# A hybrid mLSTM and attention layer on one core: output weights loaded during the attention and split during the mLSTM's first chunks

## The reference

```python
h = rmsnorm(x, norm1_w) * (1 + sc1) + sh1
mq, mk, mv, mo, mi, mf, sq, sk, sv = split_proj(h @ w_in)
...
ml_new, h_cell = mlstm_prompt(q_a, k_a, v_a, ig, lf)        # 4 heads x 128, chunkwise
y_a = rmsnorm(h_cell, ml_norm_w) * sigmoid(mo)
o_b = stick_breaking(q_b, k_all, v_all)                     # 8 heads x 64, 128-query blocks
y_b = rmsnorm(o_b, sb_out_norm_w)
mix = jnp.concatenate([y_a, y_b], axis=-1) @ w_out          # w_out: 1024 x 1024
x = x + g1 * mix
h2 = rmsnorm(x, norm2_w) * (1 + sc2) + sh2
x = x + g2 * (conv_ffn(h2) @ w_down)
```

## Time and profile before

| | |
|---|---|
| median of 3 runs (lowest to highest) | 3388.79 us (3387.54 to 3391.09) |
| the profiled execution's own time | 3391.34 us |
| its span, first to last instruction | 3389.7 us |
| mean granted TensorE clock | 0.968 of full speed |
| PE / PEld busy | 3178.1 (94%) / 2797.1 (83%) us |
| DVE / ACT / POOL busy | 1531.8 (45%) / 1076.4 (32%) / 749.2 (22%) us |
| DMA | 335.88 MB, mean 99 GB/s |

### The profile page before, as it was taken

One profiled execution on the slowest core, in us unless ns is written; L12 is line 12 of the kernel. 1 busy time (PEld: TensorE's weight loads), 2 busy tenths in 40 slices (PEclk: granted clock), 3 DMA queues, 4 the chain that ended last, 5 costly groups with the idle time before them and its releaser, 6 DMA issues. The chain is left out here.

```text
span 3389.7 us, 45737 instructions
## 1 busy us (share of the span) xinstructions
PE 3178.1 (94%) x17258; PEld 2797.1 (83%) x17258; DVE 1531.8 (45%) x1986; ACT 1076.4 (32%) x2064; POOL 749.2 (22%) x665
## 2 busy tenths in 40 slices
PE   7999999996999999896996999999999994999999
PEld 3877777774998999675885999999999994887786
DVE  1300000554988899574652544444444444324322
ACT  3611111222776777223553221222122212112111
POOL 3311101222665666001110111111111112002000
PEclk9999999997999999897997999999999997999999
DMA  5312211336522340564544111111111114335332
GB/s 184 114 66 67 68 62 66 127 125 156 133 52 52 67 83 9 185 231 178 180 159 158 50 50 50 37 38 50 50 50 50 50 38 151 139 117 173 139 138 70
DMA packets 247992, 335.88 MB, mean 99 GB/s; under 512 B 58093, under 2 KB 170153, under 8 KB 240685
## 3 DMA queue, kind: packets, MB, share of 16 engines
q1 hardware_dynamic: 231662, 284.75, 27.5%
q0 software_dynamic: 14864, 49.31, 4.4%
q10 hardware_dynamic: 1332, 0.06, 0.0%
HBM read 225.16 MB, written 108.89 MB: 99 GB/s over the span
## 5 line engine op out<-in xcount | busy, mean ns | idle before, releaser
L1770 PE MATMUL facc<-h2H,fwH 128*128 128x416 f32 x1760 | 617.8, 351 | 25.4 <-DVE h2L L1719 25.4
L1770 PE MATMUL facc<-h2L,fwH 128*128 128x416 f32 x1760 | 617.5, 351 | 0.0
L1770 PE MATMUL facc<-h2H,fwL 128*128 128x416 f32 x1760 | 617.3, 351 | 0.0
L644 PE MATMUL pacc<-pring,h1H 128*128 128x512 f32 x1360 | 453.0, 401 | 18.6 <-POOL pring L520 12.7
L941 POOL TENSOR_TENSOR aS<-aS,aC 128x512 f32<-128x512 f32 (+3 forms) x326 | 334.2, 1031 | 199.7 <-DVE aC L903 196.5
L903 DVE TENSOR_TENSOR_SCAN aC<-aB,aC,a 128x512 f32<-128x512 f32 (+3 forms) x326 | 362.7, 1113 | 24.2 <-ACT aB L878 17.8
L1662 ACT ACTIVATE fU<-facc 128x416 f32<-128x416 f32 (+1 forms) x220 | 113.1, 514 | 788.4 <-PE facc L1770 788.4
L1736 DVE TENSOR_SCALAR fV<-fU,fcw,fcb 128x2048 f32<-128x2048 f32 x88 | 112.3, 1318 | 536.8 <-ACT fU L1664 536.7
L1770 PEld LDWEIGHTS facc<-h2H,fwH 128*128 128x128 f32 x1760 | 331.1, 188 | 28.7 <-issue 26.1
L1770 PEld LDWEIGHTS facc<-h2H,fwL 128*128 128x128 f32 x1760 | 331.1, 188 | 2.7
L1770 PEld LDWEIGHTS facc<-h2L,fwH 128*128 128x128 f32 x1760 | 331.2, 188 | 2.5
(11 more groups left out here) (265 smaller groups left out, 4745.8 us busy)
## 6 DMA issues: line engine op xcount, KB each, us to landing
da<-act_d SPq DMA_DIRECT2D x32, 1408.0 KB, 7.0
proj_out<-pstage SPq DMA_DIRECT2D x119, 256.0 KB, 2.0
fraw<-w_up SPq DMA_DIRECT2D x44, 512.0 KB, 5.7
act_d<-fV SPq DMA_DIRECT2D x22, 1024.0 KB, 5.3
qk_T<-pturn POOLq DMA_DIRECT2D x68, 256.0 KB, 3.0
aq<-qk_T SPq DMA_DIRECT2D x32, 512.0 KB, 12.1
mwa<-w_ada SPq DMA_DIRECT2D x16, 1024.0 KB, 5.5
praw<-w_in SPq DMA_DIRECT2D x56, 256.0 KB, 2.8
```

The costliest lines, as they stand in the source:

```text
L644: op = mm_(acc[:, n % NB], h[:, kk, tok(t)], weight(q, w), start=(kk == 0 and part == 0), stop=(kk == KD - 1 and part == 2))
L1770: mm = nc.tensor.matmul(dst, a[:, j, kk], h[:, kk, cols], start=(kk == 0 and m == 0), stop=(kk == KD - 1 and m == 2))
```

## The change

- `w_out` becomes a tile that lives from the attention to the end of the mLSTM. In the attention its 32 KB per partition first hold `xk`, `xq` and `blank` (11 of 16 pieces). When the sync engine comes to row 0 of head 3, behind that row's store, it waits until the cached keys and queries are turned and the blank rows stored, and loads `w_out` there.
- In the mLSTM two tiles are added, `oH` and `oL`. ScalarE copies four parts ahead of its work on chunk 0 and four ahead of that on chunk 1; POOL makes four low parts ahead of its wait for chunk 0's result and four ahead of that for chunk 1's. The load of `w_out` at the end is gone, and the modulation's bias is loaded into the tile of its rows and added in place.
- The output projection gets `oH` and `oL` instead of `w_out`; its splitting and the waits for it are gone. Tile 0 is loaded first, then the norm weights, tiles 1 and 2, and last the gate rows, which have their own semaphore, waited for ahead of the first `finish`.

```diff
@@ attention
-        xq = sbuf(nc, s, "bxq", [P, W5])
-        xk = sbuf(nc, s, "bxk", [P, NPB1, W5])
+        spare = w_out[:].rearrange("p k (a n) -> p (k a) n", n=W5)
+        xk, xq, blank = spare[:, 0:NPB1], spare[:, NPB1], spare[:, NPB1 + 1]
...
                 store(scored[m])
                 if kind == PROMPT and (h, i) == (0, NPT // 2):
                     load_sample()
+                if kind == PROMPT and (h, i) == (3, 0):
+                    sp.wait_ge(turned, max(x for x in range(N) if items[x][0] in (KEYS, QUERIES)) + 1)
+                    sp.wait_ge(blank_stored, 16)
+                    sp.dma_start(w_out[:], d["w_out"].rearrange("(k p) n -> p k n", p=P)).then_inc(w_out_in, 16)
...
+            sp.wait_ge(w_out_in, 16)
@@ mlstm
-        bias = sbuf(nc, s, "mbias", [2, NM * P])
...
             tiles(sp, body)
-            sp.dma_start(w_out[:], d["w_out"].rearrange("(k p) n -> p k n", p=P)).then_inc(w_out_in, 16)
-            sp.wait_ge(w_out_in, 16)
             sp.wait_ge(mod_row, NPT)
...
             def body(t, u, r, first):
+                if isinstance(t, int) and t in (0, 1):
+                    for kk in range(t * KD // 2, (t + 1) * KD // 2):
+                        pool.wait_ge(o_high, kk + 1)
+                        nc.gpsimd.tensor_tensor(oL[:, kk], w_out[:, kk], oH[:, kk].bitcast(F32), ALU.subtract).then_inc(o_low, 1)
                 pool.wait_ge(h_ready, t + 1)
...
             def body(t, u, r, first):
+                if isinstance(t, int) and t in (0, 1):
+                    for kk in range(t * KD // 2, (t + 1) * KD // 2):
+                        nc.scalar.activation(oH[:, kk], w_out[:, kk], ACT.Copy).then_inc(o_high, 1)
                 act.wait_ge(qkv_in[u], 48 * r + 48)
...
-                v.tensor_tensor(mod_rows[:, span], pm[0:2, 0:2 * P], bias[:, span], ALU.add).then_inc(mod_row, 1)
+                v.tensor_tensor(mod_rows[:, span], pm[0:2, 0:2 * P], mod_rows[:, span], ALU.add).then_inc(mod_row, 1)
@@ output_projection
-            for n in range(2):
-                src = d["mods"][n:n + 1, (2 * KD - NMOD) * P:(3 * KD - NMOD) * P]
-                sp.dma_start(gate[:, n], src.to_broadcast([P, D])).then_inc(rows_in, 16)
-            sp.dma_start(wrow[:], d["y_norms"]).then_inc(rows_in, 16)
...
-            for t in range(3):
+            load(Turn(0, 0, 0))
+            sp.dma_start(wrow[:], d["y_norms"]).then_inc(rows_in, 16)
+            for t in range(1, 3):
                 load(Turn(t, t, 0))
+            for n in range(2):
+                src = d["mods"][n:n + 1, (2 * KD - NMOD) * P:(3 * KD - NMOD) * P]
+                sp.dma_start(gate[:, n], src.to_broadcast([P, D])).then_inc(gate_in, 16)
             turns_of_four(sp, slot)
...
-            for kk in range(0, KD, 2):
-                weights_split(pool, kk)
...
-            for kk in range(KD):
-                nc.scalar.activation(wH[:, kk], raw[:, kk], ACT.Copy).then_inc(w_high, 1)
...
-            dve.wait_ge(rows_in, 48)
-
-            for kk in range(1, KD, 2):
-                weights_split(dve, kk)
+            dve.wait_ge(rows_in, 16)
...
+                if first(i):
+                    dve.wait_ge(gate_in, 32)
                 dve.wait_ge(mix_ready, i.t + 1)
...
-                        if isinstance(i.t, int) and i.t == 0 and half == 0:
-                            pe.wait_ge(w_low[kk % 2], kk // 2 + 1)
```

More of the change, by code:

```diff
@@ L710, in _, with attention @@
                 turn(m)
-def attention(k, c):
+def attention(k, c, w_out):
     nc, d = k.nc, k.d
@@ L737, in attention @@
     (edge_set, nought_set, z_ready, pass_ready, stop_ready, left_ready, w_ready, turned, av_done, o_taken, past_k_in, past_v_in,
[L738 removed]
+     sample_set, sample_stored, blank_stored, w_out_in) = k.sems(
         "edge_set", "nought_set", "z_ready", "pass_ready", "stop_ready", "left_ready", "weight_ready", "weight_turned",
[L740 removed]
+        "av_done", "o_taken", "past_k_loaded", "past_v_loaded", "sample_tiles_set", "sample_stored", "blank_stored",
+        "w_out_loaded")
     taken = [k.sem("turned_taken_by_act"), k.sem("turned_taken_by_dve")]
@@ L821, in load_sample @@
                 own = tok(NPT)
-                sp.dma_start(xq[:], d["proj_out"][5, own, :]).then_inc(past_k_in, 16)
+                sp.dma_start(xq, d["proj_out"][5, own, :]).then_inc(past_k_in, 16)
                 for x, g, cache, sem in ((xk, 6, "past_k", past_k_in), (vs, 3, "past_v", past_v_in)):
@@ L932, in _ @@
             nc.gpsimd.memset(qs[:], 0.0).then_inc(sample_set, 1)
-            nc.gpsimd.memset(blank[:], 0.0).then_inc(sample_set, 1)
+            nc.gpsimd.memset(blank, 0.0).then_inc(sample_set, 1)
             nc.gpsimd.tensor_copy(far_s[:], c["far_r"][:, 0:DEC].bitcast(F32).unsqueeze(1).to_broadcast([P, 4, DEC])
@@ L1004, in _, with mlstm @@
                 scores(av, n - 6)
-def mlstm(k, c, gc, dec, w_out):
+def mlstm(k, c, gc, dec, w_out, oH, oL):
     nc, d = k.nc, k.d
@@ L1070, in _ @@
             sp.dma_start(C[1][:], d["c_init"]).then_inc(state_in, 16)
-            sp.dma_start(bias[:], d["b_ada"][:, NMOD * P:].to_broadcast([2, NM * P])).then_inc(bias_in, 16)
+            sp.dma_start(mod_rows[:], d["b_ada"][:, NMOD * P:].to_broadcast([2, NM * P])).then_inc(bias_in, 16)
             def body(t, u, r, first):
@@ L1301, in _, with output_projection @@
             mm.then_inc(mod_turned, 1)
-def output_projection(k, c, raw):
+def output_projection(k, c, wH, wL):
     nc, d = k.nc, k.d
@@ L2011, in build @@
         k.end_phase()
-        attention(k, c)
-        k.end_phase()
         with ExitStack() as s:
             w_out = sbuf(nc, s, "w_out_sb", [P, KD, D])
-            mlstm(k, c, gc, dec, w_out)
+            attention(k, c, w_out)
             k.end_phase()
-            output_projection(k, c, w_out)
+            oH = sbuf(nc, s, "w_out_high", [P, KD, D], F32R)
+            oL = sbuf(nc, s, "w_out_low", [P, KD, D], F32R)
+            mlstm(k, c, gc, dec, w_out, oH, oL)
+            k.end_phase()
+            output_projection(k, c, oH, oL)
             k.end_phase()
```

18 lines of the change are left out of this document (5 added, 13 removed).

## The result

The changed kernel takes **3404.55 us** (median of 8 runs, 3397.37 to 3408.79), the kernel before in the same comparison 3389.89 (8 runs, 3387.54 to 3391.47). The ratio is 1.0041, with a 95% interval of 1.0030 to 1.0051: slower, by some 14.7 us. The forecast was 3391.2 with a range to 3398.5, and "the same" as the likeliest case. It was wrong.

What follows compares the result with a forecast made beforehand. The prediction took TensorE's pace to bound each stage once going. Its terms, -5.9 + 5.5 + 2.8 = +2.4 us, made the profiled 3391.34 into 3393.7, and the median 3388.79 into 3391.2 us; range 3383.5 to 3398.5.

Steps and rivals of the forecast that it cites:

- Term 1: Output projection's start: splitting gone and tile 0 loaded first bring the first product earlier, -5.9 us (bounds 4.4 to 6.9).
- two things were late: tile 0, behind 1.57 MB of row constants, and VectorE: Projection's start: tile 0 arrives behind other loads, and VectorE's weight subtractions end 1.5 us behind its statistics.
- Term 2: Attention: the weights' load delays a store, VectorE's copy of row (3,9) waits 6.4 us: +5.5 us (bounds 3.3 to 7.5).
- TensorE sets the pace afterwards, so nothing is won back: Attention, after the copy's wait: the delay stays as it is, leaving the cost at +5.5 us.
- Term 3: mLSTM's start: ScalarE's copies, a slow clock and POOL's subtractions cost 0.75 + 1.0 + 1.0 = +2.8 us (bounds 0.75 to 6).
- Its first two parts: mLSTM, chunk 1: ScalarE's copies make the keys 0.75 us late; the new hole prolongs the 1.2 GHz clock, costing 1.0.
- I find 2.7 us of holds: mLSTM: POOL's second four subtractions hold VectorE operations 2.7 us; with 1.8 to spare, about 1.0 reaches TensorE.
- The one on the slower side: mLSTM: each of POOL's second four subtractions holds a VectorE operation, 10.8 us in all; total 3399.2 us, chance 0.13.
- That the store isn't held: Attention: the small store slips through the large load's gaps, no wait; total 3385.7 us, chance 0.16.
- a projection of only -3: Projection: starts only 3 us earlier, tile 0 sharing DMA engines with loads issued behind it; 3394.1 us, chance 0.07.

Runs made afterwards that it cites:

- order_only: The kernel before, with only tile 0's loads first and the gate rows last on their own semaphore, splitting left in the projection: 3388.13 us, ratio 0.9995.
- load_half: The changed kernel with 2 MB of the w_out load behind row 0 of head 3 and 2 MB behind row 8: 3395.27 us.
- load_late: The changed kernel with the w_out load behind row 8 of head 3 instead of row 0: 3393.53 us, ratio 1.0011.
- ring16: The changed kernel, load still behind row 0 of head 3, with sixteen attention output tiles instead of eight: 3393.65 us.
- two_behind: load_late with six POOL subtractions ahead of the store of chunk 0's h and two behind it, instead of four and four: 3382.13 us.
- pool_pieces: load_late with each POOL subtraction cut into four pieces of 256 columns: 3397.30 us.
- store_last: load_late with POOL's second four subtractions ahead of the store of chunk 0's h, behind the same wait: 3387.66 us.
- store_gap: load_late with POOL's second four subtractions waiting until the store of chunk 0's h has landed: 3387.81 us.
- dve_low: The changed kernel with the load behind row 8, ScalarE's copies behind its value copy, all subtractions on VectorE in the projection: 3382.85 us, ratio 0.9983.
- early_table: dve_low with a one-column square root as ScalarE's first instruction of the projection: 3382.52 us, ratio 0.9978.
- pool_paced: load_late with POOL waiting for the end of each of its subtractions before the next: 3385.56 us, ratio 0.9990.
- act_gap: load_late with ScalarE's weight copies behind its value copy in chunks 0 and 1 instead of ahead of the key scaling: 3392.61 us.

## Why the prediction was wrong, point by point

**Term 1, the projection (-5.9): right, -6.3.** Arrival, statistics and first product lie within 0.6 us of their forecasts. Its step "two things were late: tile 0, behind 1.57 MB of row constants, and VectorE" holds, but they are no sum: order_only took the first away and gained nothing.

**Term 2, the attention (+5.5): the mechanism right, the size wrong, +12.1.** Load, wait (7.44 for 6.4) and hole (6.11 for 5.5) lay in the bounds. The step that failed is "TensorE sets the pace afterwards, so nothing is won back", which stops at the hole. A hole of this length also took the clock: 6.0 us more. The prediction priced the clock in the mLSTM, where its rows showed a slow one, and not here, where 6 us of idleness were forecast in a stage at 2.4 GHz. That left out 6.0 of the 6.6 us by which the term was short. load_half, with a third of the hole and none of the slow clock, shows that a short hole costs its length alone. load_late and ring16 show that nothing else cost time here. The Trainium skill has the rule on the page *TensorE: Matmul & The Clock Gate*, "What's actually happening": there are two levels, and the clock drops to the lower after idleness. The trace agrees, with 1.00 ahead of the hole and 0.50 behind it; load_half's hole of 1.90 us left it at 1.00.

**Term 3, the mLSTM's start (+2.8): +11.6.** Its first two parts, 0.75 for ScalarE and 1.0 for the clock, came to 0.7 and 1.1 from chunk 0's first product to chunk 1's scores. Their make-up differs (the hole was 2.42 us: the keys were ready 10.3 us after chunk 0's first product, for a forecast of 10.4, but TensorE, at the higher clock, was through with its work ahead of the transposes 1.8 us sooner than before); that the sum is the same is in part luck. Some 1.6 us fell at the border, in the wait for `mRU`; the twelve experiments show 9.0 to 9.8 us from the last copy to chunk 0's first product, this profile 10.6, and no run tells why. The step that failed is "I find 2.7 us of holds", of which "about 1.0 us gets through". It followed each two-input operation with blocks of 2.35 us and let it in at the next block's end. Behind a POOL store it isn't let in: one `VU` stood through the whole train of four, and TensorE's delay grew by 8.4 us, slow clock included, where 1.0 had been forecast. two_behind, pool_pieces, store_last and store_gap show the form of this; taking POOL's work away (dve_low) brings `VU` back to 0.70 us and the stretch to 184.7 us (187.2 in early_table), which is that of before, 186.0, as far as one profile tells.

**The rivals.** The one on the slower side named the right resource (POOL holds VectorE), a threshold of 7.2 us that was passed, and 10.8 us where 11.6 were measured. Its form, each subtraction catching another operation, isn't what happened, and 1.6 of the 11.6 us fell at the border, so the near size is in part luck. Its chance of 0.13 was too low. That the store isn't held is refuted by the 7.44 us wait, a projection of only -3 by the -6.3.

**The range** ended at 3398.5 because it let each term reach its bound, 7.5 and 6.0. Both were broken at once. The first was the length of one wait, with no price for what a long wait does to TensorE's clock. The second, as far as it was POOL's, was made of holds of one subtraction each, and had no room for a hold through four.

## What to carry to other kernels

A large load on a queue whose small stores free a ring stalled the ring's writer here. Put it where one turn of the ring takes longer than the load, or make the ring longer (neither cost the attention anything here). Ask what a hole on TensorE does to its clock: 1.9 us cost 2.0 here, 6.1 us cost 12.1, and nothing between them was run. And don't put a train of two-input POOL operations right behind a store that POOL issues: read the trace for slots in which ScalarE and VectorE wait anyway (VectorE for the first tile's statistics, here), and put the work there.

## What the runs showed of the hardware that was not expected

**POOL's store and the subtractions behind it.** In seven profiles of seven in which `VU` started within a POOL store's issue that subtractions followed without a gap, it ended only behind all of them. Here is load_late's, with the first subtraction shown alone:

```profile
1389.89 0.59 POOL L1117 DMA_DIRECT2D h_d<-mH  x1 [12.20 <-DVE mH L1200]
1390.11 10.21 DVE L1155 TENSOR_TENSOR mVU<-mVI,gate_cols 128x516 f32<-128x516 f32 x1
1390.50 2.35 POOL L1115 TENSOR_TENSOR w_out_low<-w_out_sb,w_out_high 128x1024 fp32r<-128x1024 f32 x1
```

The subtraction starts 0.39 us after `VU`, runs its usual 2.35 us, and the next three follow it, while `VU` stands. `VU` took 10.2 us behind four (five profiles), 5.6 behind two, 11.9 behind sixteen quarters. An operation that starts in the middle of a subtraction gets in at its end (2.85 us in store_last). Neither half is enough alone: the store without subtractions held nothing (store_gap), nor did a train that began during `qw` without a store (store_last). The prediction cited the Trainium skill, *SBUF — State Buffer*, "SBUF: two separate sides", by which the pair of ports goes for a whole instruction to whichever starts first. By the starts in these rows that would be `VU`, with no hold; the measurement decides, and it says a hold of four instructions. Why the ports aren't handed over between them was only argued and stays open, and so does whether a wait between the subtractions would do it.

**A small shift moves 9 us.** `VU` was held where it started 0.22 us into the store's issue (the changed kernel), and free where it started 0.07 us before it (pool_paced). Of the experiments with the train behind the store only pool_paced shifted the two, by a wait on POOL itself; those with edits further ahead (load_half, ring16, act_gap) kept the 0.22. A gain that comes with such a shift is not yet the edit's.
